# FFN up products: high weight half against both operand halves in one 512-column matmul, the sums added on VectorE

## The reference

```python
def rms_norm(x, g):            # x * rsqrt(mean(x*x) + eps) * g
def swiglu(h, w13, w2):        # w13: 1024 x 5632, w2: 2816 x 1024
    a, b = split(h @ w13, 2)   # "up": two halves of 2816
    return (silu(a) * b) @ w2  # "down"
...
x = x + 0.5 * swiglu(rms_norm(x, ffn1_norm[l]), ffn1_w13[l], ffn1_w2[l])   # 4 of these in all
...
mod = silu(c) @ w_mod[l] + b_mod[l]       # second stack: shifts, scales and gates
```

## Time and profile before

| | |
|---|---|
| median of 3 runs | 1620.63 us (1620.55 to 1701.14) |
| profiled execution | 1621.52 us, span of its instructions 1619.6 us |
| TensorE clock granted, mean | 0.985 of full |
| busy: PE, PEld, DVE, ACT | 1563.9, 1506.2, 1182.8, 783.4 us |
| share of the chain that ended last: PE, DVE, ACT | 79%, 2%, 1% |
| L1613, L1619, L1620 on the chain | 23% each |

### The profile page before, as it was taken

The page is one execution under the profiler, slowest core; times in us unless marked ns, Lnnn a source line. Parts: engine busy times, 40 slices in busy tenths (PEclk is TensorE's granted clock), DMA queues, the critical chain, the costliest instruction groups (busy, mean ns, idle before and its releaser), DMA issues.

```text
span 1619.6 us, 29914 instructions
## 1 busy us (share of the span) xinstructions
PE 1563.9 (97%) x12334; PEld 1506.2 (93%) x12334; DVE 1182.8 (73%) x1658; ACT 783.4 (48%) x1117; POOL 9.9 (1%) x14
## 2 busy tenths in 40 slices
PE   7999997999999999999899999999989999889999
PEld 7999997999999899999679999987689999789999
DVE  6887788878778678887767877774777877576564
ACT  6434458543445434445655343542654444445452
POOL 0000000000000000000000000000000000000000
PEclk9999998999999999999999999999999999999999
DMA  6666642556665337655233766632236676245550
GB/s 264 236 249 237 260 161 105 208 185 250 232 242 198 141 142 274 252 221 218 89 114 122 264 257 242 261 123 86 98 131 235 258 273 249 79 157 182 183 183 27
DMA packets 43450, 311.10 MB, mean 192 GB/s; under 512 B 4816, under 2 KB 5072, under 8 KB 6096
## 3 DMA queue, kind: packets, MB, share of 16 engines
q1 hardware_dynamic: 41904, 303.33, 50.0%
q0 software_dynamic: 864, 5.21, 0.9%
q10 hardware_dynamic: 576, 1.05, 0.2%
HBM read 308.52 MB, written 1.05 MB: 191 GB/s over the span
## 4 chain that ended last, share of the span: by engine, by line
PE 79%; DVE 2%; issue 1%; ACT 1%; DVEq 0%; ACTq 0%
PE psum L1613 23%; PE psum L1619 23%; PE psum L1620 23%; PE psum L1686 1%; PE psum L1798 1%; PE psum L1786 1%; PE psum L1990 1%; PE psum L1996 1%; PE psum L1995 1%; PE psum L2121 1%; PE psum L2132 0%; PE psum L2047 0%; PE psum L1913 0%; PE psum L2010 0%; PE psum L1593 0%
## 5 line engine op out<-in xcount | busy, mean ns | idle before, releaser
L1613 PE MATMUL psum<-u_hi,w_hi 128*128 128x256 f32 (+1 forms) x2544 | 733.4, 288 | 23.9 <-DVE u_lo L1267 10.9
L1619 PE MATMUL psum<-u_lo,w_hi 128*128 128x256 f32 (+1 forms) x2544 | 723.7, 284 | 0.0
L1620 PE MATMUL psum<-u_hi,w_lo 128*128 128x256 f32 (+1 forms) x2544 | 723.1, 284 | 0.0
L911 DVE TENSOR_TENSOR w_lo<-raw,w_hi 128x1024 fp32r<-128x1024 f32 x480 | 565.6, 1225 | 120.9 <-ACT w_hi L452 120.5
L452 ACT ACTIVATE w_hi<-raw 128x1024 fp32r<-128x1024 f32 x480 | 478.2, 1047 | 104.2 <-PE psum L1613 91.0
L1613 PEld LDWEIGHTS psum<-u_hi,w_hi 128*128 128x128 f32 x2544 | 491.0, 193 | 31.2 <-issue 16.1
L1619 PEld LDWEIGHTS psum<-u_lo,w_hi 128*128 128x128 f32 x2544 | 491.2, 193 | 0.7 <-issue 0.2
L1620 PEld LDWEIGHTS psum<-u_hi,w_lo 128*128 128x128 f32 x2544 | 491.0, 193 | 0.0
L1613 PE MATMUL psum<-hid_hi,w_hi 128*128 128x256 f32 x1220 | 348.2, 285 | 12.1 <-issue 11.6
L1619 PE MATMUL psum<-hid_lo,w_hi 128*128 128x256 f32 x1220 | 346.8, 284 | 0.0
L1620 PE MATMUL psum<-hid_hi,w_lo 128*128 128x256 f32 x1220 | 346.7, 284 | 0.0
(11 more groups left out here) (229 smaller groups left out, 977.0 us busy)
## 6 DMA issues: line engine op xcount, KB each, us to landing
raw<-stream SPq DMA_DIRECT2D x288, 1024.0 KB, 4.9
buf<-tab POOLq DMA_DIRECT2D x2, 768.0 KB, 5.2
x<-x_in SPq DMA_DIRECT2D x1, 1024.0 KB, 7.0
buf<-ctx_in POOLq DMA_DIRECT2D x1, 1024.0 KB, 5.4
buf<-poolmat POOLq DMA_DIRECT2D x1, 1024.0 KB, 5.7
out<-x ACTq DMA_DIRECT2D x4, 256.0 KB, 2.1
cst<-consts POOLq DMA_DIRECT2D x1, 864.0 KB, 9.7
buf<-late POOLq DMA_DIRECT2D x1, 640.0 KB, 4.1
```

The source lines that it names most:

```text
L911: ve.tensor_tensor(w_lo[:, u], raw[:, u], w_hi[:, u].bitcast(F32), ALU.subtract).then_inc(S.lo_ready, 1)
L1613: ins = te.matmul(dst, w_hi[:, w], hi, start=first, stop=False, skip_group_check=True)
L1619: te.matmul(dst, w_hi[:, w], lo, start=False, stop=False, skip_group_check=True)
L1620: return te.matmul(dst, w_lo[:, w], hi, start=False, stop=last, skip_group_check=True)
```

## The change

The tiles `u_hi` and `u_lo` become `um` and `us`. In `um` a block's first 256 columns hold the main operand's high half, its last 256 columns the low half, side by side (but for the MLPs, the pooling and the mixed products of the second stack, whose low half goes to `us`); side-path operands go to `us`. The up products of steps 2 to 21 of the four FFNs use the new `wide_k`; those of steps 0 and 1, the down products, and all other stages keep three matmuls of 256 columns. `UP_BANK` gives steps from 2 on two banks each, 6 and 7 for even steps, 4 and 5 for odd ones. `hidden(j)` from step 2 on has an ACT copy and a DVE addition more. DVE works the modulation units inside `hidden` instead of after the splits, and PE's sum of a group moves to the middle of the up products of the next step, with waits of its own, since bank 6 is in use now. The loop on PE is written out.

```diff
-        MOD_ACC[_g] = _i % 2 if _name == "mlp0" else int(_i >= len(_groups) - 3)
+        MOD_ACC[_g] = _i % 2
...
-UP_BANK = [4, 5, 7] + [4 + _j % 2 for _j in range(3, FFS)]
+UP_BANK = [4, 5] + [6 - 2 * (_j % 2) for _j in range(2, FFS)]
...
-        u_hi_t = sb("u_hi", NC * 2 * T, F32R)
-        u_lo_t = sb("u_lo", NC * 2 * T, F32R)
+        um_t = sb("um", NC * 2 * T, F32R)
+        us_t = sb("us", NC * 2 * T, F32R)
...
+        t_lo = buf5[:, 1024:1536]
...
 # ACT, hidden(j)
+                    if j > 1:
+                        act.wait_ge(S.up_ready, h0 + j + 1)
+                        sc.activation(t_lo.rearrange("p (k t) -> p k t", k=2), psum[:, UP_BANK[j]:UP_BANK[j] + 2, T:2 * T],
+                                      ACT.Copy).then_inc(S.up_lo, 1)
                     act.wait_ge(S.up_scaled, h0 + j + 1)
...
 # DVE, swiglu
-                def hidden(j):
-                    dve.wait_ge(S.up_ready, h0 + j + 1)
-                    ve.tensor_tensor(t2.rearrange("p (k t) -> p k t", k=2), bank2(UP_BANK[j]), over2(rstd[:, :]),
-                                     ALU.mult).then_inc(S.up_scaled, 1)
+                def hidden(j, mods=0):
+                    t = t2.rearrange("p (k t) -> p k t", k=2)
+                    if j > 1:
+                        dve.wait_ge(S.up_lo, (FFS - 2) * FFNS[name] + j - 1)
+                        link(ve.tensor_tensor(t, psum[:, UP_BANK[j]:UP_BANK[j] + 2, 0:T], t_lo.rearrange("p (k t) -> p k t", k=2),
+                                              ALU.add))
+                        ve.tensor_tensor(t, t, over2(rstd[:, :]), ALU.mult).then_inc(S.up_scaled, 1)
+                    else:
+                        dve.wait_ge(S.up_ready, h0 + j + 1)
+                        ve.tensor_tensor(t, bank2(UP_BANK[j]), over2(rstd[:, :]), ALU.mult).then_inc(S.up_scaled, 1)
+                    if mods:
+                        pump_to(nxt[0])
                     dve.wait_ge(S.gated, h0 + j + 1)
                     ve.tensor_tensor(h32[:, 0:T], sil, t2[:, T:2 * T], ALU.mult).then_inc(S.hid_f32, 1)
+                    if mods > 1:
+                        pump_to(nxt[0])
                     dve.wait_ge(S.hid_hi_ready, h0 + j + 1)
...
+                mods = 0
                 for j in range(FFS - 2):
-                    hidden(j)
-                    pump_to(unit_at(name, "down", j) - 1)
-                    if j in SUM_AT[name]:
-                        read_modulation(HOME[name][SUM_AT[name].index(j)])
+                    if j - 1 in SUM_AT[name]:
+                        read_modulation(HOME[name][SUM_AT[name].index(j - 1)])
+                    hidden(j, mods)
+                    mods = MODS_AT[name][j + 2]
+                    pump_to(unit_at(name, "down", j) - 1 - mods)
...
-                hidden(FFS - 2)
+                hidden(FFS - 2, mods)
...
 # PE
+            def wide_k(c, dst):
+                unit_ready(c)
+                for k in range(NC):
+                    w = slice((c % RING) * UNIT + k * P, (c % RING) * UNIT + (k + 1) * P)
+                    ins = te.matmul(dst, w_hi[:, w], um[:, k, :], start=k == 0, stop=False, skip_group_check=True)
+                    if begun[0] != c:
+                        ins.then_inc(S.unit_used, 1)
+                        begun[0] = c
+                    ins = te.matmul(dst[:, 0:T], w_lo[:, w], um[:, k, 0:T], start=False, stop=k == NC - 1, skip_group_check=True)
+                return ins
...
+                def up(j):
+                    c, b = unit_at(name, "up", j), UP_BANK[j]
+                    if j > 2:
+                        pe.wait_ge(S.up_scaled, h0 + j - 1)
+                    if j - 2 in SUM_AT[name]:
+                        pe.wait_ge(S.mod_read, groups[SUM_AT[name].index(j - 2)] + 1)
+                    wide_k(c, psum[:, b, :])
+                    if j - 1 in SUM_AT[name]:
+                        g = groups[SUM_AT[name].index(j - 1)]
+                        pe.wait_ge(S.up_scaled, h0 + j)
+                        sum_modulation(g, MOD_ACC[g], last_unit(g))
+                    wide_k(c + 1, psum[:, b + 1, :]).then_inc(S.up_ready, 1)
...
-                with pe.Fori(0, (FFS - 10) // 4) as i:
-                    for s in range(4):
...
+                for j in range(2, FFS):
+                    up(j)
...
```

More of the change, by code:

```diff
@@ L146 @@
 ATT_PUMP = [AT["wo"] + 4, AT["wo"] + 6] + [AT["ffn3"] + _g for _g in range(6)]
-UP_BANK = [4, 5, 7] + [4 + _j % 2 for _j in range(3, FFS)]
+UP_BANK = [4, 5] + [6 - 2 * (_j % 2) for _j in range(2, FFS)]
+FFNS = {"ffn0": 0, "ffn1": 1, "ffn2": 2, "ffn3": 3}
 MOD_COL = 300
@@ L481, in gain_operand @@
                     for k in (2 * b, 2 * b + 1):
-                        sc.activation(u_hi[:, k, 0:T], x[:, k, :], ACT.Identity, scale=col(gain, k))\
+                        sc.activation(um[:, k, 0:T], x[:, k, :], ACT.Identity, scale=col(gain, k))\
                           .then_inc(S.operand_hi, 1)
@@ L537, in mlp_operand @@
                 for k in (2 * b, 2 * b + 1):
-                    sc.activation(u_hi[:, k, 0:T], x[:, k, :], ACT.Identity, scale=ty(gain, k)).then_inc(S.operand_hi, 1)
+                    sc.activation(um[:, k, 0:T], x[:, k, :], ACT.Identity, scale=ty(gain, k)).then_inc(S.operand_hi, 1)
                 square(NRM[name], x_t, b)
@@ L1671, in diagonal_block @@
                         ins = product(bank2(b0 + n)[:, mo, :], c, ((n % 2) * 4 + kk * 2 + mo) * P,
-                                      u_hi[:, k, t0:t0 + T], u_lo[:, k, t0:t0 + T], kk == 0 and mo == 0, kk == 1,
+                                      *operands(k), kk == 0 and mo == 0, kk == 1,
                                       begins=None if begins is None else begins * (kk == 0 and mo == 0))
@@ L1716, in swiglu @@
                     by_chunk(c0, name, first[:2], S.up_ready)
-                    up(c0 + 2, 0, 1, UP_BANK[1], h0)
+                    all_k(c0 + 2, 0, first[2])
+                    all_k(c0 + 3, 0, first[3]).then_inc(S.up_ready, 1)
                 else:
@@ L1720, in swiglu @@
                 norm_sum(norm)
-                for j in range(2, 10):
-                    up(unit_at(name, "up", j), 0, j, UP_BANK[j], h0)
+                for j in range(2, FFS):
+                    up(j)
                     if j == 2:
                         pe.wait_ge(S.ms_ready, NRM[norm] + 1)
-                    down(j - 2, (j - 2) % 4, unit_at(name, "down", j - 2), first=j == 2)
-                    if j in SUM_AT[name]:
-                        g = groups[SUM_AT[name].index(j)]
-                        sum_modulation(g, 0, last_unit(g))
-                with pe.Fori(0, (FFS - 10) // 4) as i:
-                    for s in range(4):
-                        j, c = 10 + 4 * i + s, unit_at(name, "up", 10 + s)
-                        up(c, 2 * i, j, 4 + s % 2, h0)
-                        down(j - 2, s, c + 3, 2 * i)
-                        if s == 2:
-                            sum_modulation(groups[-3] + i, 1, unit_at(name, "mod", 13), 2 * i)
-                down(FFS - 2, (FFS - 2) % 4, end_of(name) - 2)
+                    down(j - 2)
+                down(FFS - 2)
                 if name in ("ffn0", "ffn1"):
                     sum_context(int(name[3]))
-                down(FFS - 1, (FFS - 1) % 4, end_of(name) - 1, last=True)
+                down(FFS - 1)
             def sqrelu(name, norm):
@@ L1986, in token_product @@
             def token_product(dst, c, at, k, tt, first, last):
-                w, t = slice((c % RING) * UNIT + at, (c % RING) * UNIT + at + 512), slice(tt * P, (tt + 1) * P)
-                ins = te.matmul(dst, u_hi[:, k, t], w_hi[:, w], start=first, stop=False)
+                w, t = slice((c % RING) * UNIT + at, (c % RING) * UNIT + at + 512), (tt % 2) * P
+                hi, lo = (m[:, k, t0:t0 + P] for m in [um if tt < 2 else us] for t0 in (t, T + t))
+                ins = te.matmul(dst, hi, w_hi[:, w], start=first, stop=False)
                 if begun[0] != c:
@@ L1994, in token_product @@
                     begun[0] = c
-                te.matmul(dst, u_hi[:, k, t], w_lo[:, w], start=False, stop=False)
-                return te.matmul(dst, u_lo[:, k, t], w_hi[:, w], start=False, stop=last)
+                te.matmul(dst, hi, w_lo[:, w], start=False, stop=False)
+                return te.matmul(dst, lo, w_hi[:, w], start=False, stop=last)
             dftc = buf5[:, 1024:1024 + 2 * P]
```

105 lines of the change are left out of this document (52 added, 53 removed).

## The result

The changed kernel takes 1629.05 us (median of 8 runs, 1628.46 to 1630.59). The kernel before, run beside it, takes 1625.38 us (median of 8; most of its runs lie near 1620.4 or near 1625.7). One of these eight, at 1701.14 us, was in the slow state and is left out of the ratio. The ratio of the times is 1.004, interval 1.0023 to 1.0057: slower by about 0.4%; the interval lies above 1 and well under 2%. The profiled execution took 1628.46 us against 1621.52 before, its span 1626.6 against 1619.6.

A forecast was written before the change was run, and what follows sets the result against it. PE was taken as the bound, never waiting in the FFNs; 17.0 us gained against 19.9 us of new waits, net +2.9, gave 1623.5 us, range 1608 to 1638.

The forecast's parts named there:

- wide matmul, 1280 blocks: FFN up products: block 0.360 to 0.347 us, 13.3 ns less, 17.0 us gained; bounds 4 and 34 us.
- start of each FFN, 4: Before down(1) of each FFN: PE waits 0.5 us for the split and loses 0.2; 2.8 us in all.
- doubled modulation, ffn0 and ffn1: ffn0 and ffn1: DVE passes of 9.25 us against PE steps of 8.43; 6.4 us of PE waiting.
- context steps and end, ffn2: ffn2: copy queued behind the context operand, passes 9.65, 6.2 us; last down waits 1.6 and some 1.3 more.
- end, ffn3: ffn3's last down: PE waits 1.6 us for hidden(21), which DVE reaches late.
- if wide matmuls stand 0.235 apart: PE's up products: a sign that the forecast is wrong; wide matmuls were expected 0.227 us apart.
- The skill's 2.5 ns: Up products: by the skill's rule, one matmul less saves 2.5 ns, 3 us in all; the forecast used 13 ns.
- The waits in the middle of `up`: PE's modulation sum within up(j): in time at lag 1.6 us with doubled modulation, so no wait.
- Edits at nothing: Moved operands, bank pairs and written-out loop cost nothing; without queue cover, 48 unrolled steps could cost a few tenths each.
- everything hides: Rival, chance 0.20: DVE and ACT keep ahead in the FFNs; 1603.6 us, up to 1612 with start and end waits.
- the wide matmul gains nothing: Rival, chance 0.10: over 13 ns beside the 512 columns; PE gains 4 us, waits 15; 1632 us.
- DVE is late in every modulation step: Rival, chance 0.14: single-modulation pass above 8.65 us makes DVE the bound; 1634 us at 0.3 beyond.

The follow-up runs named there:

- e9: Kernel after, second (context) modulation accumulation left out for three of four units of the doubled groups; 1622.18 us, one run.
- e6: Kernel after with hidden(21) of each FFN put ahead of the last four splits on DVE and ACT; ratio to kernel before 1.0031.
- e1: Kernel after with wide matmuls kept but ACT's copy and DVE's addition left out (product incomplete); ratio to kernel before 0.9938.
- e3: Kernel after with each wide matmul split into two of 256 columns, copy and addition kept; ratio to kernel before 1.0068.
- e4: Kernel after with a unit's eight 512-column matmuls issued first, then its eight 256-column ones; ratio to kernel before 1.0021.
- e2: Kernel after with three 256-column matmuls a block again, no copy or addition, other edits kept; ratio to kernel before 1.0012.
- e8: Kernel after with ACT's copy kept and waited for, DVE's addition left out (product incomplete); ratio to kernel before 0.9906.

## Why the prediction was right, and where not

The sign and the mechanism were right, and the measured time lies in the range. The net was too low by 5 us in the FFNs (+2.9 forecast, +7.9 measured), which is two errors, of 7.3 and of 2.2 us, that partly cancel. It would be luck to take the medians for a hit: 1629.05 less 1625.38 is 3.7, near the 2.9, only because the median of the kernel before lies on the upper of its two levels; the profiled spans differ by 7.0. By stages, ffn2 came out as said (+5.8, about 5 forecast), ffn0 and ffn1 a little worse (+1.0, near equal forecast), and ffn3 missed: about 2 us shorter was forecast, +0.14 measured.

| term | forecast | measured | from |
|---|---|---|---|
| wide matmul, 1280 blocks | -17.0 | -9.7 | spacing in the kernel after |
| start of each FFN, 4 | 2.8 | about 2.1 | gap and late down(1) |
| doubled modulation, ffn0 and ffn1 | 6.4 | about 5.1 | e9 |
| context steps and end, ffn2 | 9.1 | 7.7 | what is left of ffn2 |
| end, ffn3 | 1.6 | 1.7 | e6 |
| rest | 0 | about 1 | 0.5 of it the gain of `up(2)`, ahead of the stages |
| sum of the waits | 19.9 | 17.7 | stage lengths and spacing |

- **The bound** was read rightly: PE is full in the FFNs before, so a cut of PE counts (e1) and a wait counts in full (e3).
- **The gain of the wide matmul is the term that was mis-sized.** The step that failed is "I take 17.0, since the 0.227 spacing is the regular one". A price in one pattern (512 columns behind 512) was carried to another (512 and 256 in turn), where it is 235.6 and 116.7. The other end of the bound, 3 ns, came from 0.237 and a narrow one at 0.120; 7.6 lies between the two, and "if wide matmuls stand 0.235 apart" stood among the signs that the forecast is wrong: by that sign this term was. e4 shows that the pattern is the cause of about half, 2.8 of 5.7 ns, and by place in the row that the first five of a row are slow and the others at 227, as in the token products. So 0.227 was a right price for a pattern that the kernel after does not have. The spacing hardly depends on whether DVE or ACT works beside it: 235.6 ns with DVE at work, 236.6 without; 236.0 with ACT, 235.0 without. Why a 512-column matmul behind a 256-column one is slower stays open.
- **The skill's 2.5 ns** (the Trainium skill, TensorE: Matmul & The Clock Gate, Back-to-back issue gap: the isolated gap of one warm matmul is the columns over 2.4 GHz and 2.5 ns) would make the gain 3 us; e1 gained 8.8 in the stages, and 10 to 22 ns stand beside the columns here, so the trace doesn't agree.
- **The waits** came where they were put, and the passes of DVE to 0.01 and 0.06 us (9.24 for 9.25, 9.59 for 9.65, 8.04 for 8.05). In sum they are 2.2 us shorter than forecast. One reason is that PE's own step is 8.52 and not 8.43, so each late pass falls 0.09 less behind: 24 passes (two FFNs of doubled modulation, one of context steps) times 0.09 are 2.2. e3 bears that out: with the same list for DVE and a step of 8.64, the FFNs' waits are 14.0 us in place of 17.7, 3.7 less for 0.12 us a step; scaled down, 0.09 is worth some 2.8, an estimate. The two shorter context passes are worth another 0.5. The waits in the middle of `up`, which the prediction put at nothing, are late passes of DVE met at another place; no run tells their share apart.
- **The end of ffn2 and ffn3**: 12.65 for 12.8, waits of 2.6 and 1.6 for 2.9 and 1.6.
- **Edits at nothing**: right, e2 differs by 0.02 us in the sum. The few tenths that the prediction names for each written-out step, should the cover go, are shown by no run.
- **The rivals.** That everything hides is refuted by e8: without the addition the FFNs are 16 us shorter than with it. That the wide matmul gains nothing is refuted by e1; its condition, more than 13 ns beside the 512 columns, came true in part: 22 ns, where the rival's 3 ns of gain needed 24. That DVE is late in every modulation step is refuted by ffn3 (+0.14) and e9. The whole time alone would have hidden the answer: 1629.05 lies nearer to the 1632 of the "no gain" case than to the 1623.5 of the forecast, and only the stages and e1 tell the two apart.

## What to carry to other kernels

A matmul's price beside its columns depends on what stands next to it: take it from rows in the pattern that the change will have, also by the place in the row, and where there are none, keep both ends, because a few ns times a thousand instructions decide how such a trade comes out. An engine that is 77% busy on average can be the bound in some steps: sum its own list of work for each kind of step, waits for other engines included, and compare it with the step of the engine that leads. Where a trade pays in some steps only, make it in those steps alone; a wait that is moved out of a stage can come back at the next boundary, as most of e6's did.
